# Reordering five joins of a two-block transformer kernel: key tiles side by side, reciprocals in parts, latents rounded block by block

## The reference, cut to what matters

```
# first block: attention on q, k, v, and a gated linear unit, both from one input projection
q = rms_norm(q) ; k = rms_norm(k)                       # 16 query heads, 4 key heads, width 128
y_a = windowed_gqa(q, k, v, sink)
y_b = (y_act @ glu_w_a) * sigmoid(y_act @ glu_w_b)
# second block, even layer: a convolution branch and 8 heads on latents of width 512, then a post-norm
kv = rms(kv_latent) @ w_kvb ; q = rms(q_latent) @ w_qb   # per head softmax(q k) v, for x and for a context
z = ALPHA * x + gate * y ; x = (z - mean(z)) * rsqrt(var(z) + eps) * g + b
# second block, odd layer: the next projection reads x * (1 + scale) + shift
k = rms(x_in @ w_k) ; ...
```

## Time and profile before

| what | value |
|---|---|
| time, median of 3 runs | 4141.28 us (4135.25 to 4151.66) |
| profiled execution: its time, its span | 4163.41 us, 4161.6 us |
| TensorE busy | 3924.3 us, 94% of the span |
| VectorE busy | 2397.8 us, 58% |
| ScalarE busy | 1655.4 us, 40% |
| GpSimd busy | 843.1 us, 20% |
| granted TensorE clock, mean | 0.975 |
| chain that ended last, by engine | TensorE 78%, VectorE 13%, ScalarE 4%, issue 3% |

### The profile page before, as it was taken

How to read it: one execution, slowest core, us unless ns; L and a number is a source line. 1 busy time by engine, 2 the same in 40 slices (tenths; PEclk the granted TensorE clock), 3 DMA queues, 4 the chain that set the end, 5 groups by cost and what they waited for, 6 DMA issues and landing times.

```text
span 4161.6 us, 72950 instructions
## 1 busy us (share of the span) xinstructions
PE 3924.3 (94%) x30180; PEld 3600.3 (87%) x30180; DVE 2397.8 (58%) x3403; ACT 1655.4 (40%) x2312; POOL 843.1 (20%) x611
## 2 busy tenths in 40 slices
PE   7999998899999988999999999999999888989997
PEld 6777678899999988999999999999999556768887
DVE  5999966542777767555555555533232333657546
...
DMA packets 132292, 679.31 MB, mean 163 GB/s; under 512 B 43664, under 2 KB 49936, under 8 KB 52368
## 3 DMA queue, kind: packets, MB, share of 16 engines
...
## 4 chain that ended last, share of the span: by engine, by line
PE 78%; DVE 13%; ACT 4%; issue 3%; POOL 1%; DMA 1%; ACTq 0%; DVEq 0%; POOLq 0%
PE banks L409 50%; PE banks L2147 17%; DVE w_lo L387 1%; PE banks L2267 1%; PE banks L2061 1%; DVE pq L1270 1%; DVE banks L1260 1%; PE banks L2323 1%; ACT w_hi L379 1%; PE banks L2216 1%; DVE rq L1306 1%; PE banks L2215 1%; DVE banks L1247 1%; ACT gw L712 1%; PE banks L2389 1%
## 5 line engine op out<-in xcount | busy, mean ns | idle before, releaser
L409 PE MATMUL banks<-h_hi,w_hi 128*128 128x256 f32 (+1 forms) x6176 | 1663.0, 290 | 96.8 <-DVE w_lo L387 37.3
L409 PE MATMUL banks<-h_hi,w_lo 128*128 128x256 f32 (+1 forms) x6176 | 1641.1, 286 | 0.0
L409 PE MATMUL banks<-h_lo,w_hi 128*128 128x256 f32 (+1 forms) x6176 | 1640.4, 286 | 0.0
L379 ACT CAST w_hi<-ring 128x1024 fp32r<-128x1024 f32 x986 | 984.2, 1048 | 1029.1 <-PE banks L409 453.3
L387 DVE TENSOR_TENSOR w_lo<-ring,w_hi 128x1024 fp32r<-128x1024 f32 x798 | 995.4, 1279 | 635.6 <-ACT w_hi L379 632.5
L409 PEld LDWEIGHTS banks<-h_hi,w_hi 128*128 128x128 f32 x6176 | 1123.3, 191 | 166.0 <-issue 118.8
L409 PEld LDWEIGHTS banks<-h_hi,w_lo 128*128 128x128 f32 x6176 | 1115.5, 190 | 15.7 <-issue 0.5
L409 PEld LDWEIGHTS banks<-h_lo,w_hi 128*128 128x128 f32 x6176 | 1115.9, 190 | 15.0
L387 POOL TENSOR_TENSOR w_lo<-ring,w_hi 128x1024 fp32r<-128x1024 f32 x188 | 480.9, 2558 | 1692.8 <-ACT w_hi L379 1691.2
L2147 PE MATMUL banks<-wp_hi,w_hi 128*128 128x256 f32 x2048 | 566.9, 277 | 6.7 <-DVE wp_lo L1539 3.4
L2147 PE MATMUL banks<-wp_hi,w_lo 128*128 128x256 f32 x2048 | 566.6, 277 | 0.0
...
## 6 DMA issues: line engine op xcount, KB each, us to landing
...
```

What stands on the lines that cost most here:

```text
L379: act.copy(w_hi[:, t.par, s], weights(t.slot)[:, s]).then_inc(hi_done, 1)
L409: m = pe.matmul(bank(b, e - a, a), w[:, t.par, k], x(k)[:, a:e], start=first and a == 0, stop=last and e == n, skip_group_check=e - a < n)
```

## The change

It has five parts, in the order of the program.

1. In the gate phase `heads_scaled` is cut in two. `key_scaled` takes the reciprocal of rows 0 and 1 of `rq5` and scales the key head, at even tiles. `queries_scaled` takes that of rows 2 to 4 and scales the queries, at the odd tile behind it, after that tile's `lo_split`.
2. In the glu phase the product of a pair (`glu_pair`) moves from the end of the odd head to the next even head, behind that head's largest value and `o_read`. ScalarE's rounding of the attention output (`o_hi`) moves from heads 5, 9, 13 to 6, 10, 14.
3. The last `agate` tile raises `h2_freed` after every second block, and the rounding of the latents follows it block by block. The `agate` loops are written out.
4. In the heads on latents the last piece of the next head's scores is issued behind the turn of this head.
5. At the post-norm VectorE makes all 16 low parts, and GpSimd subtracts the mean of chunks 12 to 15 from the moment that the mean is known. The second key tile is split before the norm's chunks, both low halves by VectorE, and TensorE multiplies each chunk with both key tiles up to chunk 10, then finishes the first tile, then the second.

```diff
@@ -391,7 +391,7 @@
-def dense(pe, t, xh, xl, n=T, b=None, before={}, width=None):
+def dense(pe, t, xh, xl, n=T, b=None, before={}, width=None, after=None):
@@ -408,6 +408,8 @@
                               stop=last and e == n, skip_group_check=e - a < n)
+        if after is not None and k % 2 and k < BLK - 1:
+            m.then_inc(after, 1)
     m.then_inc(mm_done, 1)
@@ -642,7 +644,7 @@
             act.activation(sg[:, h // 2 % 2], bank(t.bank()), ACT.Sigmoid).then_inc(S("sg_ready"), 1)
-        if h in (5, 9, 13):
+        if h in (6, 10, 14):
             o_hi(h // 4 - 1)
@@ -830,14 +832,15 @@
         act.activation(cvg[:], bank(tg.bank()), ACT.Silu).then_inc(S("cvg_ready"), 1)
-    with act.Fori(0, 2, 1) as i:
-        for j in range(4):
-            t = Tile("agate", j, i, 4)
-            hi_split(act, t.next())
-            act.wait_ge(mm_done, t.done())
-            act.activation(mx[:, i * 4 + (j + 8)], bank(t.bank()), ACT.Silu).then_inc(acc_free[t.bank()], 1)
-    for q in range(4):
-        act.copy(lh[:, 2 * q:2 * q + 2], lat[:, 2 * q:2 * q + 2]).then_inc(S("lh_done"), 1)
+    for j in range(8):
+        t = Tile("agate", j)
+        hi_split(act, t.next())
+        if j == 7:
+            for q in range(4):
+                act.wait_ge(S("h2_freed"), q + 1)
+                act.copy(lh[:, 2 * q:2 * q + 2], lat[:, 2 * q:2 * q + 2]).then_inc(S("lh_done"), 1)
+        act.wait_ge(mm_done, t.done())
+        act.activation(mx[:, j + 8], bank(t.bank()), ACT.Silu).then_inc(acc_free[t.bank()], 1)
     def m_exp(n):
@@ -922,6 +925,8 @@
         square(15)
+        if layer == 0:
+            hi_split(act, Tile("k1", 1))
         mean(1, D)
@@ -932,7 +937,7 @@
         if k >= 4:
-            act.wait_ge(S("h2_pool") if k % 2 == 0 else S("h2_ready"), (k - 4) // 2 + 9)
+            act.wait_ge(S("h2_ready"), 8 + k - 3)
         for s_ in range(2):
@@ -959,7 +964,7 @@
-    for j in range(4):
+    for j in range(1, 4):
         hi_split(act, Tile("k1", j).next())
@@ -1074,11 +1079,11 @@
             lo_split(pool, Tile("aout", j, i, 4).next(), 0)
-    for k in range(0, 16, 2):
-        pool.wait_ge(S("hm_hi"), 16 + k + 1)
-        pool.tensor_tensor(h2_lo[:, k], hmr[:, k % 4], h2_hi[:, k].bitcast(F32), ALU.subtract)\
-            .then_inc(S("h2_pool"), 1)
-    for j in range(8):
+    pool.wait_ge(S("ln_mean"), 2)
+    for k in range(12, 16):
+        pool.tensor_tensor(XX[:, k], XX[:, k], lnm[:], ALU.subtract).then_inc(S("h2_pool"), 1)
+    pool.wait_ge(lo_done[0], N0["k1"] + 2)
+    for j in range(1, 8):
         lo_split(pool, Tile("k1", j).next(), 0)
@@ -1300,11 +1305,15 @@
-    def heads_scaled(g):
+    def key_scaled(g):
         dve.wait_ge(S("root5"), g + 1)
-        L(dve.reciprocal(rq5[:], rq5[:]))
+        L(dve.reciprocal(rq5[:, 0:2], rq5[:, 0:2]))
         dve.scalar_tensor_tensor(qku[:, 16 + g], qku[:, 16 + g], V("kg"), rq5[:, 0], ALU.mult, ALU.mult)
+    def queries_scaled(g):
+        L(dve.reciprocal(rq5[:, 2:5], rq5[:, 2:5]))
         q = qku[:, 4 * g:4 * g + 4]
@@ -1319,8 +1328,8 @@
                     .then_inc(S("ya_ready"), 1)
-        if j in (2, 4, 6, 8):
-            heads_scaled(j // 2 - 1)
+        if 2 <= j < 10:
+            (key_scaled, queries_scaled)[j % 2](j // 2 - 1)
         if j == 10:
@@ -1332,6 +1341,17 @@
         dve.tensor_copy(qku[:, h], bank(7, T)).then_inc(S("o_ready"), 1)
+    def glu_pair(p):
+        ta, t = Tile("glu", 2 * p), Tile("glu", 2 * p + 1)
+        dve.wait_ge(S("sg_ready"), p + 1)
+        L(dve.tensor_tensor(sg[:, p % 2], sg[:, p % 2], bank(ta.bank()), ALU.mult))
+        dve.sem_inc(acc_free[ta.bank()], 1)
+        dve.sem_inc(acc_free[t.bank()], 1)
+        g = gates[:, 16 + 2 * p:18 + 2 * p]
+        dve.tensor_tensor(g, g, sg[:, p % 2].rearrange("p (a t) -> p a t", a=2), ALU.mult)\
+            .then_inc(S("glu_done"), 1)
@@ -1350,6 +1370,8 @@
             o_read(h - 2)
+            if h % 2 == 0:
+                glu_pair(h // 2 - 1)
         dve.wait_ge(S("exp_done"), h + 1)
@@ -1357,18 +1379,9 @@
         lo_split(dve, t.next(), 1)
-        if h % 2:
-            p = h // 2
-            ta = Tile("glu", h - 1)
-            dve.wait_ge(S("sg_ready"), p + 1)
-            L(dve.tensor_tensor(sg[:, p % 2], sg[:, p % 2], bank(ta.bank()), ALU.mult))
-            dve.sem_inc(acc_free[ta.bank()], 1)
-            dve.sem_inc(acc_free[t.bank()], 1)
-            g = gates[:, 16 + h - 1:16 + h + 1]
-            dve.tensor_tensor(g, g, sg[:, p % 2].rearrange("p (a t) -> p a t", a=2), ALU.mult)\
-                .then_inc(S("glu_done"), 1)
         if h in (6, 10, 14):
             o_lo(h // 4 - 1)
+    glu_pair(HEADS // 2 - 1)
     o_read(HEADS - 2)
@@ -1664,6 +1677,10 @@
         dve.wait_ge(S("lh_done"), q + 1)
+        if q < 3:
+            dve.wait_ge(S("h2_freed"), q + 5)
+        else:
+            dve.wait_ge(mm_done, G0["agate"] + 8)
         s_ = slice(2 * q, 2 * q + 2)
@@ -1775,12 +1792,16 @@
         dve.sem_inc(S("ln_acc"), 1)
+        if layer == 0:
+            lo_split(dve, Tile("k1", 1), 1)
...
             .then_inc(S("ln_acc"), 1)
+        if layer == 0:
+            lo_split(dve, Tile("k1", 1), 0)
         dve.wait_ge(S("ln_root"), 1 + layer)
@@ -1789,24 +1810,28 @@
-        def lo_odd(k):
+        def low(k):
             dve.wait_ge(S("hm_hi"), 16 + k + 1)
...
+        own = 16 if layer else 12
         ahead = shift(0)
             shifted = ahead
-            if k < 15:
+            if k + 1 < own:
                 ahead = shift(k + 1)
-            dve.wait_ge(chain.sem, shifted)
+            if k < own:
+                dve.wait_ge(chain.sem, shifted)
+            else:
+                dve.wait_ge(S("h2_pool"), 8 + k - 11)
             x = XX[:, k, 0:n]
             dve.tensor_tensor(x, x, lnr[:, 1, 0:n], ALU.mult).then_inc(S("ln_done"), 1)
-            if layer == 0 and k >= 4 and k % 2 == 0:
-                lo_odd(k - 3)
+            if layer == 0 and k >= 2:
+                low(k - 2)
         if layer == 0:
-            lo_odd(13)
-            lo_odd(15)
+            low(14)
+            low(15)
@@ -1816,11 +1841,12 @@
     dve_out("aout", 0, N2)
-    dve.wait_ge(S("h2_ready"), 16)
+    dve.wait_ge(S("h2_ready"), 24)
...
         t = Tile("k1", j)
-        lo_split(dve, t.next(), 1)
+        if j:
+            lo_split(dve, t.next(), 1)
         dve.wait_ge(mm_done, t.done())
@@ -2201,13 +2227,12 @@
             dense(pe, Tile("conv", j, i, 4, skip=4), xh2, xl2, N2, width=T)
-    with pe.Fori(0, 2, 1) as i:
-        for j in range(4):
-            dense(pe, Tile("agate", j, i, 4), xh2, xl2, N2, width=T)
-    def m_scores(n):
+    for j in range(8):
+        dense(pe, Tile("agate", j), xh2, xl2, N2, width=T, after=S("h2_freed") if j == 7 else None)
+    def m_scores(n, pieces=range(4)):
         hp = slice(64 * (n % 2), 64 * (n % 2) + 64)
-        for b in range(4):
+        for b in pieces:
             if n and b < 3:
@@ -2280,8 +2305,10 @@
             if n % 4 < 3:
-                m_scores(n + 1)
+                m_scores(n + 1, range(3))
             m_turn(n)
+            if n % 4 < 3:
+                m_scores(n + 1, range(3, 4))
             m_values(n)
@@ -2304,13 +2331,28 @@
-    def next_wait(k):
-        sem, c = (S("h2_ready") if k % 2 else S("h2_pool")), 8
-        return lambda: pe.wait_ge(sem, c + k // 2 + 1)
     pe_out("aout", 0, N2)
-    for j in range(4):
-        dense(pe, Tile("k1", j), xh2, xl2, N2, before={} if j else {k: next_wait(k) for k in range(16)})
+    def k_part(t, k):
+        for n, (w, x) in enumerate(((w_hi, h2_hi), (w_lo, h2_hi), (w_hi, h2_lo))):
+            m = pe.matmul(bank(t.bank()), w[:, t.par, k], x[:, k], start=(k + n == 0), stop=(k == 15 and n == 2))
+        return m
+    t0, t1 = Tile("k1", 0), Tile("k1", 1)
+    for t in (t0, t1):
+        pe.wait_ge(acc_free[t.bank()], t.bank_free())
+        wait_weights(pe, t)
+    for k in range(16):
+        pe.wait_ge(S("h2_ready"), 8 + k + 1)
+        m = k_part(t0, k)
+        if k < 11:
+            k_part(t1, k)
+    m.then_inc(mm_done, 1)
+    for k in range(11, 16):
+        m = k_part(t1, k)
+    m.then_inc(mm_done, 1)
+    for j in range(2, 4):
+        dense(pe, Tile("k1", j), xh2, xl2, N2)
     def v1_tile(j):
         wait_weights(pe, t)
```

## The result

In one measurement with 19 runs of each kernel, the changed kernel takes 4121.15 us (median; 4100.41 to 4149.35) and the kernel before 4151.66 (4131.81 to 4188.74). The ratio is 0.9927, with a 95% interval from 0.9903 to 0.9951: a gain of 30 us, between 20 and 40. The forecast was a gain of 44 and a time of 4097, in a range from 4078 to 4118; the time is 3 us above the range. The profiled execution of the changed kernel took 4119.14 us, with a span of 4117.3. The ratios of all measurements here leave out the executions that stand far off: one of 4203.87 us of the kernel before, timed beside experiments 5 to 8, and one of 5525.07 us in experiment 16.

What follows compares the result with a forecast made beforehand. TensorE, busy 94% of the span, was taken as the bound, with time gained only at its waits or low clock. Terms 1.8 + 21.0 + 7.6 + 5.5 + 12.0 = 47.9, set to 44: 4141.3 - 44 = 4097 us, range 4078 to 4118.

Steps and rivals of the forecast that it cites:

- Part 1, the reciprocals: Gate phase: cutting the reciprocal moves TensorE's wait from one tile to the next; a gain of 1.8 us, not 14.
- rival (a): Gate phase: GpSimd comes first, costing 2.4 us in three groups; part 1 loses 5.5, time 4104; chance 0.17.
- Part 4 and the clock behind it: Heads on latents: the last scores piece covers waits of 0.77 us; 2.8 gained per half, 5.5 together.
- Rival (e): Slower than before: half clock through the heads on latents; falling in the second half costs some 22 us; chance 0.02.
- Part 2: Glu: exponential starts 2.01 us earlier in seven pairs, less 1.3, plus 8.2 from returning clock; gain 21.0.
- rival (b): Glu and latents: the clock stays as it is, 8.2 and 2.6 less, 37 gained, time 4104; chance 0.15.
- Part 3: Latents: TensorE starts 5.0 us earlier and 2.6 of clock loss comes back; gain 7.6.
- Part 5: Post-norm key tiles: first low part at 3648.0, first two tiles done at 3676.7 instead of 3688.6; gain 12.0.
- Rival (c): New key loop: VectorE or TensorE is slower there; sum 36 or less, time 4105 to 4110; chance 0.06.
- The base: Whole kernel: timed runs taken as 4141.3 us, 22.1 shorter than the profiled execution's 4163.4.
- The 3.9 us that I took off: Whole kernel: a third of the 10.8 us of counted-back clock, likely missing in timed runs; 47.9 became 44.

Runs made afterwards that it cites:

- experiment 5: Changed kernel with the reciprocals cut at one row: the key's row alone, then the four rows of the queries; ratio 0.9898, gate phase 70.9 us.
- Experiment 6: Kernel before with only the latents rounded block by block; ratio 0.9991.
- experiment 7: Kernel before with only the two key tiles side by side and the low parts and mean subtractions that feed them; ratio 0.9962.
- 8: Changed kernel with the reciprocal whole again and unread matmuls in TensorE's waits at both entries of the latent heads; ratio 0.9844, median 4096.16 us.
- experiment 16: Changed kernel with two unread matmuls behind the last head of the first half; ratio 0.9944.
- experiment 1: Kernel before with only glu's pair product and the rounding of the attention output moved; ratio 0.9958.
- 9: Changed kernel with the block-by-block rounding of the latents undone; ratio 0.9924.
- experiment 10: Changed kernel with unread matmuls at the entry of the first half of the latent heads only; ratio 0.9894.
- 4: Changed kernel with unread matmuls in TensorE's waits at both entries of the latent heads; ratio 0.9876, median 4096.78 us.
- 11: Changed kernel with two unread matmuls at the entry of the second half of the latent heads only; ratio 0.9871.
- 12: Kernel before with only the unread matmuls at both entries of the latent heads; ratio 0.9943.
- 13: Kernel before with one unread matmul behind the last head of the first half; ratio 1.0032.

## Why the prediction was wrong

The direction was right, and most terms were. The forecast counted 47.9 us against the profile and set 44; the change gives 33.4 in the profiles and 30 by time. Two terms and the base make the difference.

**Part 1, the reciprocals: the first step that failed.** The prediction had VectorE's scaling begin at 5.59 and GpSimd's low part at 5.63 after the rounding, and took the case in which VectorE "is first it keeps its place". The times were right to the digit: 634.31 and 634.35 in the changed kernel. The consequence was wrong. GpSimd got the port and the scaling took 2.71 us in three groups. That is rival (a), with the order that it named turned round: it priced this at -5.5, and the profile gives -4.9. The waits went where they were said to go, to tile 4 and then tile 5 of the gate phase:

```profile
618.69 0.35 PE L409 MATMUL banks<-h_hi,w_hi 128*128 128x256 f32 x1 [1.34 <-DVE w_lo L387]
...
631.16 0.55 PE L409 MATMUL banks<-h_hi,w_hi 128*128 128x256 f32 x1 [6.58 <-DVE w_lo L387]
```

The error is 6.7 us., which rival (a) leaned on, could not decide this: there GpSimd had begun 1.45 us ahead of VectorE. What was wrong was to let 0.04 us decide at all. In the run of the earlier trace rows it is GpSimd that is recorded first, by 0.02 us, while VectorE's operation before was still running, and GpSimd that then stood still:

```profile
3646.41 6.03 POOL L1079 TENSOR_TENSOR h_lo<-hmr,h_hi 128x512 fp32r<-128x512 f32 x1 [23.12 <-ACT h_hi L944]
3646.43 0.68 DVE L1804 TENSOR_TENSOR XX<-XX,lnr 128x512 f32<-128x512 f32 x1
```

So recorded starts this close don't tell which engine gets the ports. The Trainium skill, page "SBUF — State Buffer", section "Who interferes with whom", has the ports lent to whoever issues first; by the recorded starts this case doesn't show that, though 0.04 us may be less than what such records resolve. Nor did a gain come without the collision in experiment 5 (70.9 against 70.7), though that is another cut than the one that I had priced at 1.8.

**Part 4 and the clock behind it: the second step that failed.** The mechanism was right: 0.77 is gone in three of four heads, and at full clock a half takes 44.7 us instead of 47.95, 3.25 where 2.8 was charged. But the prediction took over the clock of each half from before ("nowhere in the heads on latents, with waits of 0.77, does the clock fall once it is up"). The first half stayed at half clock for 32 of its 60 us, and the second joined it for 24: 55.9 us instead of 44.7. Both halves together take 115.65 us, where before they took 111.6: a loss of 4.0 where 5.5 were forecast as gain. The error is 9.5 us. Rival (e) had the place and an upper price of 22 us, but its 2 in 100 were for a kernel slower than before; a fall in the second half alone had no term and no chance. The changed kernel's 19 executions, at 0.974 to 0.976, give no sign of a lucky one among them. In the profiles, all eleven of kernels that alter anything from the latents to the second entry, and leave that entry's wait as it is, have it; of the three that alter nothing there (before, and experiments 1 and 7), none. But each of these is one execution.

**Part 2** was forecast at 21.0 and gives 22.2. The waits before odd tiles are mostly 0.9 to 1.1 (0.85 forecast), odd tiles start 16.6 to 16.8 apart (16.6 forecast), and the clock came back whole, so rival (b) is out. That the clock comes back with the lower waits was an inference from one profile; none of the twelve profiles with the new order has half clock in glu, experiment 1's included.

**Part 3** was forecast at 7.6 and gives 7.6: the wait is 1.39, and 2.56 us come from the clock behind it. Experiment 6 shows that by itself it gains nothing that the time can tell.

**Part 5** was forecast at 12.0 and gives 12.5. TensorE's wait and the seams, in the changed kernel:

```profile
3603.50 6.50 POOL L1084 TENSOR_TENSOR XX<-XX,lnm 128x512 f32<-128x512 f32 x4 [12.03 <-ACT lnm L917]
...
3614.63 0.69 DVE L1815 TENSOR_TENSOR h_lo<-hmr,h_hi 128x512 fp32r<-128x512 f32 x1 [0.47 <-ACT h_hi L949]
...
3615.47 0.76 PE L2338 MATMUL banks<-h_hi,w_hi 128*128 128x512 f32 x1 [10.97 <-DVE h_lo L1815]
...
3644.12 0.40 PE L409 MATMUL banks<-h_hi,w_hi 128*128 128x512 f32 x1
```

Counted from TensorE's last statistics matmul (3604.50), the first key matmul comes at 10.97 and the third tile at 39.6; the forecast's 3648.0 and 3676.7 are 11.4 and 40.1 behind its 3636.6. Before, the third tile stood at 52.2. Rival (c) is out. GpSimd's four subtractions took 6.50 us, not the 5.2 I had charged, and still ended before VectorE came to those chunks.

**The base.** I took 4141.3 as the kernel's time, and the profile's 22.1 us above it as a sign of low clock that the timed runs don't have. Over 19 runs its median is 4151.66, and in later measurements 4149 to 4154. Three runs of a kernel whose runs spread by 57 us say too little. From 4151.7 the forecast gain would have given 4108, and the measured 33.4 give 4118 against the 4121 that were timed. The 3.9 us that I took off for this had a wrong reason: glu's low clock was in all six profiles of the old order, for 17 us in three of them and 7 in the others.

**What stays open.** Why the second half kept full clock in the profiled execution of before, behind a wait of 2.78 us, and loses it in the altered kernels. Part 3 alone has the fall (experiment 6), and so have parts 1, 2, 4 and 5 together (9); part 4 alone and part 1 alone were not run. The first half's clock is not what decides (experiment 10: full clock, and the second half falls). Matmuls in the entry wait prevent the fall in every profile that has them, in the second half (4, 8, 11) and in the first (4, 8, 10, 12); that the wait alone is not enough is seen in before.

A rival that no run here rules out is that the kernel before falls there too, in some of its executions. Of its 104 executions timed beside the experiments, 20 have a mean clock of 0.969 to 0.972, as in the profiles of experiments 6 and 13 that have the fall, and their median is 4167 us; 70 have 0.974 to 0.976, with 4147. Experiment 7's executions fall into two groups in the same way. No execution of before or of experiment 7 with the lower clock was profiled, so where its half clock lay is not known. If it lay in the second half, the altered kernels have always what before has at times. That the moment of the wait decides was a guess that my runs did not test, since they did not move it.
